# Two blocks of a hybrid model on one core: reads, weight splits, waits and output banks reordered at eight places

## The reference

```python
def first_block(...):
    ada = silu(c) @ w_ada + b_ada
    shift, scale, gate = split(ada, 3)
    h = rmsnorm(x, norm_w) * (1 + scale) + shift
    z_ssm, xbc, dt_raw, q, k, v, z_att, f_logit, g_logit = split(h @ w_in)
    y_ssm = ssd_branch(z_ssm, xbc, dt_raw, ...)   # conv, silu, 8 chunks of 128 with a carried state, rmsnorm(y * silu(z))
    y_att = fox_branch(q, k, v, z_att, f_logit)   # 8 heads of 128, causal softmax with forget sums, times silu(z)
    g_ssm, g_att = split(sigmoid(g_logit + b_gate), 2)
    merged = g_ssm * (y_ssm @ w_proj_ssm) + g_att * (y_att @ w_proj_att)
    return rmsnorm(x + gate * (merged @ w_out), final_norm_w)

def second_block(x, ...):
    z = rmsnorm(x, norm_g) @ w_in                 # columns of the three branches
    y_a = band_chunk_attention(...) * silu(ag)    # 6 heads of 64
    y_b = sigmoid(mo) * head_rmsnorm(mlstm(...)) * silu(mg)
    y_c = head_rmsnorm(gla(q, k, v, log_alpha)) * silu(gg)      # 4 heads, chunks with a carried state
    return rmsnorm(x + concat([y_a, y_b, y_c]) @ w_out, final_g)
```

## Time and profile before

| | |
|---|---|
| median of 3 runs | 1992.8 us (1992.77 to 1994.89) |
| the profiled execution | 1991.95 us, its span 1990.4 us |
| mean granted TensorE clock | 0.983 |
| TensorE matmul | 1893.3 us, 95% of the span |
| TensorE weight load | 1529.3 us, 77% |
| VectorE | 1166.6 us, 59% |
| ScalarE | 785.9 us, 39% |
| GpSimd | 161.8 us, 8% |
| `w_lo` split, one (L265, x96) | 1224 ns |
| `w_hi` split, one (L261, x96) | 1053 ns |
| landing of `acs_bc` from issue, least and most | 15.7 and 18.3 us |

### The profile page before, as it was taken

The page is one execution under the profiler, slowest core; times in us unless marked ns, Lnnn a source line. Parts: engine busy times, 40 slices in busy tenths (PEclk is TensorE's granted clock), DMA queues, the critical chain, the costliest instruction groups (busy, mean ns, idle before and its releaser), DMA issues. The chain is left out here.

```text
span 1990.4 us, 26401 instructions
## 1 busy us (share of the span) xinstructions
PE 1893.3 (95%) x9508; PEld 1529.3 (77%) x9508; DVE 1166.6 (59%) x1492; ACT 785.9 (39%) x1198; POOL 161.8 (8%) x319
## 2 busy tenths in 40 slices
PE   6998999999999999999999999699999998999997
PEld 4777778778787888888888888477777777887786
DVE  6676444555356777777776444587233335664865
ACT  5424244244224444444453333252344444442322
POOL 1000010110000000000000100012100001110100
PEclk9999999999999999999999999899999999999999
DMA  8541765543421212122215633323311111211202
GB/s 276 212 77 33 112 101 107 103 143 122 148 85 53 75 54 53 43 74 74 74 53 191 201 127 103 127 57 97 104 37 30 34 32 43 64 43 59 95 30 95
DMA packets 169154, 181.21 MB, mean 91 GB/s; under 512 B 10994, under 2 KB 143530, under 8 KB 168298
## 3 DMA queue, kind: packets, MB, share of 16 engines
q1 hardware_dynamic: 155024, 130.69, 20.7%
q0 software_dynamic: 13760, 49.30, 11.4%
q10 hardware_dynamic: 282, 0.09, 0.0%
HBM read 139.56 MB, written 40.50 MB: 90 GB/s over the span
## 5 line engine op out<-in xcount | busy, mean ns | idle before, releaser
L298 PE MATMUL acc<-ha_hi,w_hi 128*128 128x512 f32 x640 | 259.6, 406 | 5.6 <-ACT stash L311 4.4
L298 PE MATMUL acc<-ha_hi,w_lo 128*128 128x512 f32 x640 | 251.5, 393 | 0.0
L298 PE MATMUL acc<-ha_lo,w_hi 128*128 128x512 f32 x640 | 251.0, 392 | 0.0
L281 PE MATMUL acc<-ha_hi,w_hi 128*128 128x512 f32 x592 | 189.4, 402 | 29.0 <-DVE ha_lo L2172 13.6
L281 PE MATMUL acc<-ha_lo,w_hi 128*128 128x512 f32 x592 | 186.3, 396 | 0.0
L281 PE MATMUL acc<-ha_hi,w_lo 128*128 128x512 f32 x592 | 185.5, 395 | 0.0
L281 PEld LDWEIGHTS acc<-ha_hi,w_hi 128*128 128x128 f32 x592 | 111.6, 192 | 60.1 <-issue 16.4
L265 DVE TENSOR_TENSOR w_lo<-w_raw,w_hi 128x1024 fp32r<-128x1024 f32 x96 | 117.5, 1224 | 63.2 <-ACT w_hi L261 60.0
L298 PEld LDWEIGHTS acc<-ha_hi,w_hi 128*128 128x128 f32 x640 | 121.4, 190 | 30.7 <-issue 6.5
L298 PEld LDWEIGHTS acc<-ha_hi,w_lo 128*128 128x128 f32 x640 | 121.0, 189 | 26.7
L298 PEld LDWEIGHTS acc<-ha_lo,w_hi 128*128 128x128 f32 x640 | 121.4, 190 | 22.9
(11 more groups left out here) (489 smaller groups left out, 3673.0 us busy)
## 6 DMA issues: line engine op xcount, KB each, us to landing
w_raw<-in_w_in SPq DMA_DIRECT2D x99, 512.0 KB, 4.3
acs_bc<-acs_scr POOLq DMA_DIRECT2D x8, 1024.0 KB, 16.3
w_raw<-in_w_out SPq DMA_DIRECT2D x11, 512.0 KB, 3.9
x_tok<-in_x SPq DMA_DIRECT2D x8, 512.0 KB, 7.4
w_scale<-in_w_ada SPq DMA_DIRECT2D x8, 512.0 KB, 9.8
w_shift<-in_w_ada SPq DMA_DIRECT2D x8, 512.0 KB, 8.9
xt_scr<-xt SPq DMA_DIRECT2D x1, 4096.0 KB, 19.8
w_ada_g<-in_w_ada SPq DMA_DIRECT2D x8, 512.0 KB, 10.5
```

Source lines behind the costliest of these rows:

```text
L281: mm = pe.matmul(acc[:, n % 2, h * HALF:(h + 1) * HALF], w[:, n % 2, k, :], x[:, k, h * HALF:(h + 1) * HALF], start=(k == 0 and i == 0), s ...
L298: mm = pe.matmul(acc[:, 0, half * HALF:(half + 1) * HALF], w[:, n % 2, k, :], x[:, k, half * HALF:(half + 1) * HALF], start=(k == 0 and i ...
```

## The change

1. `project` with `after`: the passes go high-high, low weight, low moving side; the wait for `x_lo_done` stands before the last of the three only, and `x_hi_done` before the first. It is called so in four places (`N_SMALL1`, `N_MIX1`, `N_OUT1`, `N_SMALL2`).
2. Stage 1: `softplus_sums` goes behind the split of the next tile; the copy of the transposed sums and their `Exp` move from ACT's stage 2 into its stage 1, two tiles behind the transposes.
3. Stage 2: ACT reads the two halves of `N_Z` apart, the first ahead of the next split and of the first decay. In the last chunk the word that accumulator 1 is free (`acc_free[1]`) is given behind `outputs`, instead of at the end of DVE's stage.
4. Stage 4: the accumulator is multiplied by the sigmoid alone (`gated`), the split of a later weight tile follows, then `mix4` is multiplied by `rstd4` in a step of its own (`scale`). ACT's split for the third tile goes first in the stage, and DVE makes its reciprocal behind the first `gated`.
5. Stage 5: TensorE's waits for two accumulators and a low half go behind `scores(1)` of the first head; DVE's split of `N_FOX + 3` goes ahead of the last `t_lo`.
6. Stage 12, entry: the first partial product becomes `first_partial`, with the order of passes as in 1; `e_end` goes from DVE to POOL; on DVE the add of the second tile's halves and `operands(1)` go ahead of `key_args(2)` and `key_args(3)`.
7. Stage 12, chunks: POOL makes `k_dec` ahead of its wait for `go_done`; it waits for `kdec_turned`, the word that the buffer's last user is done.
8. Stage 13: token tiles 4 and 5 go into the two banks of `acc`, so that only tiles 2, 3, 6 and 7 wait for an earlier output; DVE waits for `final_g` (`rstd8_back`) ahead of the first use, not of the first add.

```diff
@@ -272,11 +272,13 @@
         if after is not None:
-            pe.wait_ge(x_lo_done, after + k + 1)
+            pe.wait_ge(x_hi_done, after + k + 1)
...
             pe.wait_ge(*rows[k])
-        passes = [(w_hi, x_hi), (w_hi, x_lo), (w_lo, x_hi)]
+        passes = [(w_hi, x_hi), (w_lo, x_hi), (w_hi, x_lo)] if after is not None else [(w_hi, x_hi), (w_hi, x_lo), (w_lo, x_hi)]
         for i, (w, x) in enumerate(passes):
+            if after is not None and i == 2:
+                pe.wait_ge(x_lo_done, after + k + 1)
@@ -797,6 +799,12 @@
                        bias=dcol(vec1, VEC1, "conv_b", t)).then_inc(conv_silued, 1)
+        if t == TOK_TILE + 2:
+            act.wait_ge(tok_turned, 1)
+            act.activation(tok_all[:, :, 1, :], work[:, 3, 0:NCHUNK * SSM_HEADS].rearrange("p (c h) -> p c h", h=SSM_HEADS),
+                           ACT.Copy)
+            act.drain()
+            act.activation(el_all[:, :, :], tok_all[:, :, 1, :], ACT.Exp).then_inc(tok_ready, 1)
@@ -843,6 +851,8 @@
         split_lo(dve, n + 1)
+        if t == P_TILE + 1:
+            softplus_sums()
@@ -871,8 +881,6 @@
             dve.tensor_copy(tok_all[:, :, 0, :], sp1["p"][:, :].rearrange("p (c r) -> p c r", r=SPR)[:, :, 0:SSM_HEADS])
-        if t == P_TILE:
-            softplus_sums()
@@ -1046,13 +1054,12 @@
 
-    act.wait_ge(tok_turned, 1)
-    act.activation(tok_all[:, :, 1, :], work[:, 3, 0:NCHUNK * SSM_HEADS].rearrange("p (c h) -> p c h", h=SSM_HEADS), ACT.Copy)
-    act.drain()
-    act.activation(el_all[:, :, :], tok_all[:, :, 1, :], ACT.Exp).then_inc(tok_ready, 1)
+    act.wait_ge(stash_saved[0], 16)
+    read_half(act, N_Z, 0, 0, stash[:, 0, :], func=ACT.Silu)
...
     exp_decay(0)
-    read_tile(0, 0)
+    read_half(act, N_Z, 1, 0, stash[:, 0, :], func=ACT.Silu)
+    act.drain().then_inc(stash_ready[0], 1)
@@ -1130,12 +1137,13 @@
         outputs(c)
+        if c + 1 == NCHUNK:
+            dve.drain().then_inc(acc_free[1], NCHUNK)
...
     split_lo(dve, N_GATT + 1)
-    dve.drain().then_inc(acc_free[1], NCHUNK)
@@ -1291,6 +1299,7 @@
     begin_stage(act, 4)
+    split_hi(act, N_MIX1 + 2)
@@ -1298,12 +1307,12 @@
 
+    sigmoid(0, 0)
     with act.Fori(0, 3) as j:
-        for b in range(2):
-            sigmoid(j, b)
-            split_hi(act, N_MIX1 + b + 2, adv=j)
-    sigmoid(3, 0)
-    split_hi(act, N_FOX)
+        sigmoid(j, 1)
+        split_hi(act, N_MIX1 + 3, adv=j)
+        sigmoid(j + 1, 0)
+        split_hi(act, N_MIX1 + 4, adv=j)
@@ -1311,26 +1320,33 @@
     dve.drain().then_inc(mix4_free, 2)
-    norm4.dve(dve, root4, rstd4)
-    dve.drain()
-    def mix(j, b):
+    def gated(j, b):
...
         dve.wait_ge(g_sigmoid, 2 * j + b + 1)
-        dve.tensor_tensor(gate4[:, b, :], gate4[:, b, :], rstd4[:, :], ALU.mult)
-        dve.drain()
...
         dve.tensor_tensor(mix4[:, b, :], acc[:, n % 2, :], gate4[:, b, :], ALU.mult).then_inc(acc_free[n % 2], 1)
+        dve.drain()
+    def scale(b):
+        dve.tensor_tensor(mix4[:, b, :], mix4[:, b, :], rstd4[:, :], ALU.mult)
...
 
+    split_lo(dve, N_MIX1 + 2)
+    gated(0, 0)
+    norm4.dve(dve, root4, rstd4)
+    dve.drain()
+    scale(0)
     with dve.Fori(0, 3) as j:
-        for b in range(2):
-            mix(j, b)
-            split_lo(dve, N_MIX1 + b + 2, adv=j)
-    mix(3, 0)
-    split_lo(dve, N_FOX)
-    mix(3, 1)
+        gated(j, 1)
+        split_lo(dve, N_MIX1 + 3, adv=j)
+        scale(1)
+        gated(j + 1, 0)
+        split_lo(dve, N_MIX1 + 4, adv=j)
+        scale(0)
+    gated(3, 1)
+    scale(1)
@@ -1571,10 +1587,6 @@
     begin_stage(pe, 5)
-    for a in range(2):
-        pe.wait_ge(acc_free[(N_FOX + 2 + a) % 2], (N_FOX + 2 + a) // 2 + 1)
-    pe.wait_ge(x_lo_done, T_BASE + 3)
@@ -1621,6 +1633,10 @@
         scores(1)
+        if not odd:
+            for a in range(2):
+                pe.wait_ge(acc_free[(N_FOX + 2 + a) % 2], (N_FOX + 2 + a) // 2 + 1)
+            pe.wait_ge(x_lo_done, T_BASE + 3)
@@ -1818,8 +1834,8 @@
     t_lo(2, t3_lo[:, :, :], quad_12[:, :, :], t3_hi[:, :, :])
+    split_lo(dve, N_FOX + 3)
     t_lo(3, t2_lo[:, :, :], quad_22[:, :, :], t2_hi[:, :, :])
-    split_lo(dve, N_FOX + 3)
@@ -2939,6 +2955,9 @@
     pool.dma_start(rstd8[:, :], root8_scr).then_inc(rstd8_back, 16)
+    pool.tensor_tensor(e_end[:, :].rearrange("p (c t) -> p c t", t=CHUNK),
+                       b_gla[:, :, CHUNK:CHUNK + 1].to_broadcast([P, NCHUNK, CHUNK]), b_now, ALU.subtract
+                       ).then_inc(own_ready, 1)
@@ -2948,10 +2967,12 @@
     for c in range(NCHUNK):
+        b = c % 2
+        if c >= 2:
+            pool.wait_ge(kdec_turned, c - 1)
+        pool.tensor_tensor(k_dec[:, b, :], at_chunk(gk_t, c), at_chunk(e_end, c), ALU.mult).then_inc(kdec_ready, 1)
...
             pool.wait_ge(go_done, c - 1)
-        b = c % 2
-        pool.tensor_tensor(k_dec[:, b, :], at_chunk(gk_t, c), at_chunk(e_end, c), ALU.mult).then_inc(kdec_ready, 1)
@@ -2969,16 +2990,28 @@
             pe.wait_ge(lo_done, counted(n) + 1)
-        if f:
-            pe.wait_ge(part_free, 2 * f - 1 + h)
+        pe.wait_ge(part_free, 2 * f - 1 + h)
         for k in range(K_EARLY):
-            if f == 0 and h == 0:
-                pe.wait_ge(x_lo_done, LO_SPLITS[13] + k + 1)
...
         mm.then_inc(mm_done if h else half_done, 1)
+    def first_partial():
+        n = N_OUT2
+        pe.wait_ge(lo_done, counted(n) + 1)
+        for k in range(K_EARLY):
+            pe.wait_ge(x_hi_done, SPLITS[13] + k + 1)
+            for i, (w, x) in enumerate([(w_hi, y2_hi[k]), (w_lo, y2_hi[k]), (w_hi, y2_lo[:, k, :])]):
+                if i == 2:
+                    pe.wait_ge(x_lo_done, LO_SPLITS[13] + k + 1)
+                for h in range(2):
+                    mm = pe.matmul(acc[:, 1, half_of(h)], w[:, n % 2, k, :], x[:, half_of(h)],
+                                   start=(k == 0 and i == 0), stop=(k == K_EARLY - 1 and i == 2))
+                    if k == K_EARLY - 1 and i == 2:
+                        mm.then_inc(mm_done if h else half_done, 1)
@@ -3013,9 +3046,9 @@
 
-    for f in range(2):
-        for h in range(2):
-            partial(f, h)
+    first_partial()
+    for h in range(2):
+        partial(1, h)
@@ -3071,7 +3104,7 @@
     act.activation(e_q[:, :], e_q[:, :], ACT.Exp).then_inc(decays_ready, 1)
-    act.wait_ge(decay_args, 2)
+    act.wait_ge(own_ready, 1)
@@ -3172,21 +3205,19 @@
     add_partial(0, 0)
-    dve.tensor_tensor(e_end[:, :].rearrange("p (c t) -> p c t", t=CHUNK), b_gla[:, :, CHUNK:CHUNK + 1].to_broadcast([P, NCHUNK, CHUNK]),
-                      b_now, ALU.subtract).then_inc(decay_args, 1)
...
     key_args(1)
-    dve.wait_ge(own_ready, 1)
+    dve.wait_ge(own_ready, 2)
...
     operands(0)
+    add_partial(1, 0)
+    operands(1)
+    split_early(N_OUT2 + 2)
     key_args(2)
-    operands(1)
+    add_partial(1, 1)
     key_args(3)
-    split_early(N_OUT2 + 2)
-    add_partial(1, 0)
-    add_partial(1, 1)
@@ -3241,7 +3272,8 @@
 TAIL = [(h, f) for h in range(2) for f in range(KT)]
-x2_banks = [work[:, 0:2, :].rearrange("p a b -> p (a b)"), work[:, 2:4, :].rearrange("p a b -> p (a b)")]
+work_banks = [work[:, 0:2, :].rearrange("p a b -> p (a b)"), work[:, 2:4, :].rearrange("p a b -> p (a b)")]
+x2_banks = work_banks + work_banks + [acc[:, 0, :], acc[:, 1, :]] + work_banks
@@ -3276,10 +3308,12 @@
         pe.wait_ge(part_free, PARTS12 + (KT if i < NT // 2 else 2 * KT))
-        if i >= 2:
+        if i in (2, 3):
             pe.wait_ge(out_ready, i - 1)
+        if i in (6, 7):
+            pe.wait_ge(out_ready, i - 3)
         for f in range(KT):
-            mm = pe.transpose(x2_banks[i % 2][:, f * P:(f + 1) * P], res[:, f, i * P:(i + 1) * P], ident[:, :])
+            mm = pe.transpose(x2_banks[i][:, f * P:(f + 1) * P], res[:, f, i * P:(i + 1) * P], ident[:, :])
@@ -3294,7 +3328,7 @@
         act.wait_ge(feat_turned, TURNED12 + i + 1)
-        act.activation(x2_sq[:, i % 2, :], x2_banks[i % 2], ACT.Square, accum_out=ss14[:, i:i + 1])
+        act.activation(x2_sq[:, i % 2, :], x2_banks[i], ACT.Square, accum_out=ss14[:, i:i + 1])
@@ -3312,12 +3346,13 @@
         dve.drain()
-        dve.scalar_tensor_tensor(out_tok[:, i, :], x2_banks[i % 2], inv14[:, i:i + 1], final_g[:, :],
+        dve.scalar_tensor_tensor(out_tok[:, i, :], x2_banks[i], inv14[:, i:i + 1], final_g[:, :],
...
 
-    dve.wait_ge(rstd8_back, 32)
...
         add_tail(t)
+        if t == KT + 2:
+            dve.wait_ge(rstd8_back, 32)
```

## The result

The changed kernel takes 1969.5 us (median of 4 runs, 1966.6 to 1972.6); beside it the kernel before took 1993.4 (1992.8 to 1994.9). The ratio is 0.988, with a 95% interval of 0.9862 to 0.9897. Four more runs of the same kernel, beside other experiments, gave 1971.0 (1968.2 to 1971.5).

A forecast was written before the change was run, and what follows sets the result against it. The prediction took TensorE as the bound, with time won only where it stands still or runs at half clock. Its terms summed to 13.1 us off the 1992.8 median, giving 1979.7 us, with a range from 1970 to 1986.

The forecast's parts named there:

- Stage 2 entry: Start of stage 2: the 4.4 us `stash` stall goes, a new one near 222 takes most back; net 0.3 us.
- The clock: TensorE, everywhere: stalls of 2.4 us or more bring half clock behind them, costing another 1.7 to 2.3 us.
- Stage 4: Stage 4: the 2.6 us stall goes, but a later gate load leaves one of 2.4; net 0.3 us.
- `k_dec`: Stage 12 chunks: six TensorE stalls of 0.54 us go; 3.2 us won.
- stage 13: Last stage: 2.0 us from the later `final_g` wait, 2.2 from token tiles in free banks; 4.2 together.
- Stage 12 entry: Start of stage 12: a stall of 3 us on `res`, a `y_lo` slowed by POOL, the 1861.85 wait gone; net 0.7 us.
- Stage 1: Stage 1: sums behind the split win 1.1 us; token copy and `Exp` put there cost 0.5.
- `acc_free[1]`: Start of stage 3: early release removes the 2.7 us stall, a low half is late next; net 1.0 us.
- the stage 5 entry: Start of stage 5: earlier split of N_FOX+3 shrinks the 2.45 us stall to about 1.6; net 2.1 us.
- the case between: Rival, whole kernel: one or two of the moved stalls are absent; 1965 to 1974 us, no chance of its own.
- the tail: `k_dec` and stage 13: 7.4 us; the rival that only this counts gave 1985.4 us, chance 0.12.
- vanishing stalls: Rival, whole kernel: stalls vanish, wholly or for the most part, instead of moving; about 1958 us, chance 0.14.

The follow-up runs named there:

- e2: Changed kernel with POOL's broadcast of `acs_bc` for chunk 1 issued behind the skip multiply of chunk 0 instead of ahead of it: 1971.4 us.
- e14: The kernel before, run and profiled once more without any change: 1993.4 us.
- e10: Kernel before with only `k_dec` ahead of `go_done`, last token tiles in free banks, `final_g` awaited before first use: 1981.0 us, ratio 0.9944.
- e1: Changed kernel with ScalarE reading the first half of N_Z behind the first decay again: 1971.1 us.
- e12: The changed kernel itself, run and profiled again without any change: 1971.0 us.
- e4: Changed kernel with `k_dec` made behind the wait for `go_done` again: 1974.0 us.
- e3: Changed kernel with stage 4 as before, ScalarE's order too: 1969.2 us.
- e7: Changed kernel with `e_end` by ScalarE alone, `e_q`'s argument behind the adds, N_GATT + 3's low half one turn earlier: 1963.7 us, 0.9856 of the kernel before.

## Why the prediction was wrong

**What bounds the kernel: right.** TensorE was the bound; everything was won or lost in its waits, its clock and its restarts.

**Stage 2 entry, 0.3 forecast, 6.0 measured: the step that failed.** Its mechanism held: the read of N_Z+2 hangs on the broadcast and on a weight that lands behind it (e2). Its arithmetic of the new landing did not. The prediction moved the whole chain by the 0.8 us by which the first decay would end earlier. Against a start of stage 2 that lies 1.1 us earlier, the split of N_Z+3 began at 213.17 + 1.1 = 214.3 instead of 218.76, 4.5 earlier. Four parts make this up. The decay ended at 193.26 + 1.1 = 194.4, not 195.0: 1.4 earlier, 0.8 of it forecast. The weight's issue stands in SP's queue behind the save of z, and that waits for ScalarE's read of N_Z; with one half read already, there was one read of 0.5 us less ahead of it. This is a queue that the prediction did not follow; whether the earlier issue helped by itself is not shown, since in e2 the landing did not follow it. The landing in the first trace was 1.4 us longer than in the two other executions of that order (e14, e10). And it is 1.2 shorter in the new order, for a reason that stays open. So the read ended 3.7 us earlier than forecast (221.81 + 1.1 = 222.9 against 226.6), the stall was 0.4 and not 4.2, and there was no half clock to take off (2.1). That is 5.8, of which TensorE's own arrival, 0.1 us later than forecast, took 0.1: the missing 5.7.

**The clock: a rule taken from too few rows.** The prediction took half clock for sure behind stalls of 2.4 us or more and at 1.7 to 2.3 us a time. The runs show a scatter. Behind 2.46 us (e1), 2.10 (e12), 2.66 (e10) and 3.25 (e4) it stayed up, behind 1.88 (e2) it fell, behind 1.91 near 47 it fell in both profiles of the changed kernel. Behind one and the same stall of 3.25 the stretch was 6.8, 3.4 or 0 us long. Charging moved stalls with it took 2.1 off stage 2 and 1.7 off stage 4 that did not come.

**Stage 4, 0.3 forecast, 2.9 and 1.9 measured.** The chain over POOL's gate load was right. In the first profile it was shorter than forecast: the load was issued 3.2 us later in the time of before (505.51 + 8.5 against 510.76), not 4.8, so the stall was 1.1 and not 2.4. In the second it was 4.2 later, with a stall of 2.1, close to the forecast. So of the 2.9 about 1 us is the luck of one execution, and the rest of the difference is the clock. The medians do not confirm the gain (e3).

**`k_dec`, 3.2 forecast, 4.65 measured, and stage 13, 4.2 forecast, 5.8 measured.** Both are terms that were mis-sized with the mechanism right. For `k_dec` the idle time was taken without the restart behind each wait (0.23 to 0.27 us, six times). In stage 13 the step of one tile was taken from two rows 1.86 us apart (1984.20 and 1986.06), and their transposes were not both done, as the prediction said: ScalarE had itself waited 0.39 us for one between them (four such steps are also 7.4 us, not 7.3). Without waits the step is 1.43 (1954.67, 1956.10), and VectorE sets it: ScalarE's own step there is 1.36.

**Stage 12 entry, 0.7 forecast, 0.1 and -1.1 measured.** The stall of 3 us on `res` and the slowed `y_lo` came as described. The Trainium skill's rule of a shared port ("SBUF — State Buffer", section "SBUF: two separate sides") bears on this: with GpSimd beside it the instruction took 2.62 us and ended at 1823.48, 1.1 us behind GpSimd's end at 1822.39, that is about its own length; without it 1.22. The runs agree with the rule. The row of the kernel before that the prediction called on fits less well: VectorE's multiply began 0.4 us ahead of GpSimd's (197.1, 197.53), so by the rule GpSimd should have waited, but VectorE's was the one that took 3.41 us. It ended 1.1 us behind GpSimd's end, as in the other case. The last entry of that term, the wait at 1861 that goes, was real; half clock for twice the assumed length (e12 and four more profiles) ate it.

**The rest held.** Stage 1, `acc_free[1]`, the stage 5 entry and the passes are within 0.7 us of their terms, the wait for `kept` came as the thing that is late next. Of the rivals, the case between (one or two moved stalls absent, 1965 to 1974) is the nearest to what happened: the stall near 222 is absent, and the tail, which no rival had larger, gave 3.1 us more. The case had no chance of its own; it was partly inside the range and partly inside the 0.14 for vanishing stalls. I took a moved stall for certain wherever a dated row of another engine stood in the way, by margins of 1 to 4 us that came from one execution.

## What to carry to other kernels

Where a gain hangs on what is late next, date the next step through every queue in front of it, the transfers' too, and treat a landing time of a single trace as uncertain (by 1.4 us here); such errors together decided between a stall of 4 us and none. Do not charge or credit half clock as a sure thing behind a stall of 2 to 3 us. A stall of half a microsecond in a loop of matmuls cost about 0.25 us more than its recorded idle time. And a helping engine is not free: GpSimd's subtraction took from VectorE what it spared it. ScalarE, with the subtraction folded into the bias of its exponential (e7), needed 2.44 us instead of one exponential of 1.04, and its trace shows no wait of TensorE on it there.
